# Three edits of order in a hybrid attention, convolution and SSD kernel: when the decay sums are loaded, when four token tiles are finished, and when dt's running sums are formed

## What is computed

```python
u = rmsnorm(h, norm_w[layer])
proj = jnp.einsum('bld,de->ble', u, w_in[layer])
(q, k, v, g_attn, c_b, c_c, c_h, g_conv, z, xbc, dt) = jnp.split(proj, IN_SPLIT_POINTS, axis=-1)
y_attn = diff_attention_branch(q, k, v, ...) * silu(g_attn)       # 4 heads
y_conv = short_conv_branch(c_b, c_c, c_h, ...) * silu(g_conv)
y_ssm = ssd_branch(z, xbc, dt, ...)                               # 4 groups of 4 heads, chunks of 128 tokens
h = h + jnp.einsum('ble,ed->bld', concatenate([y_attn, y_conv, y_ssm]), w_out[layer])
return rmsnorm(h, final_norm_w)[:, N_META:]

# in ssd_branch / ssd_scan
dt = softplus(dt_raw + dt_bias)
acum = jnp.cumsum(a * dt)                  # running sums inside each chunk
seg = acum[..., :, None] - acum[..., None, :]
lmat = jnp.exp(jnp.where(causal, seg, -inf))          # the decay matrix of a chunk
y_diag = (cb * lmat) @ xc
```

## Time and profile before

| | us |
|---|---|
| median of 3 runs (1050.49 to 1052.12) | 1050.74 |
| the profiled execution's own time | 1049.79 |
| its span, first to last instruction | 1048.1 |
| PE busy | 1013.8 (97%) |
| DVE busy | 665.6 (64%) |
| ACT busy | 401.8 (38%) |
| POOL busy | 253.8 (24%) |

### The profile page before, as it was taken

How to read it: one execution, slowest core, us unless ns; L and a number is a source line. 1 busy time by engine, 2 the same in 40 slices (tenths; PEclk the granted TensorE clock), 3 DMA queues, 4 the chain that set the end, 5 groups by cost and what they waited for, 6 DMA issues and landing times.

```text
span 1048.1 us, 16326 instructions
## 1 busy us (share of the span) xinstructions
PE 1013.8 (97%) x6177; PEld 924.9 (88%) x6177; DVE 665.6 (64%) x1327; ACT 401.8 (38%) x892; POOL 253.8 (24%) x222
## 2 busy tenths in 40 slices
PE   4999999999999999999999999999999999999996
PEld 3889989898999898989999989899999898888885
DVE  7555767557257674672576756724767646798866
ACT  6333442233444332334343222343442233544554
POOL 3012331333223312332224133222241330000002
PEclk9999999999999999999999999999999999999999
DMA  8012322221142222211422322114223203994313
GB/s 268 1 44 81 101 81 71 71 61 44 47 133 101 71 81 71 61 41 41 141 84 76 93 71 61 42 41 141 76 70 101 71 20 105 359 389 140 100 51 161
DMA packets 105945, 101.22 MB, mean 97 GB/s; under 512 B 6022, under 2 KB 79852, under 8 KB 105868
## 3 DMA queue, kind: packets, MB, share of 16 engines
q1 hardware_dynamic: 105868, 100.18, 30.0%
HBM read 79.11 MB, written 21.05 MB: 96 GB/s over the span
## 4 chain that ended last, share of the span: by engine, by line
PE 84%; DVE 7%; issue 3%; DMA 2%; ACT 2%; POOL 1%; SPq 0%; POOLq 0%; DVEq 0%; ACTq 0%
PE ps L1599 43%; PE ps L1608 13%; PE ps L1800 9%; PE ps L1584 5%; PE ps L1765 3%; DVE lm_buf L1433 2%; PE ps L1814 2%; DMA acum_b<-acum_scratch 2%; PE ps L1743 2%; PE ps L1744 2%; PE ps L1816 1%; PE ps L1820 1%; PE ps L1691 1%; PE ps L1766 1%; DMA conv_u<-in_norm_w 1%
## 5 line engine op out<-in xcount | busy, mean ns | idle before, releaser
L1599 PE MATMUL ps<-u_hi,w_hi 128*128 128x348 f32 (+3 forms) x1024 | 364.4, 356 | 6.7 <-ACT conv_b_s L1053 2.5
L1599 PE MATMUL ps<-u_lo,w_hi 128*128 128x348 f32 (+3 forms) x1024 | 348.3, 340 | 0.0
L1599 PE MATMUL ps<-u_hi,w_lo 128*128 128x348 f32 (+3 forms) x1024 | 347.7, 340 | 0.0
L1599 PEld LDWEIGHTS ps<-u_hi,w_hi 128*128 128x128 f32 x1024 | 194.0, 189 | 19.8 <-issue 5.5
L904 POOL TENSOR_TENSOR w_lo<-w_raw,w_hi 128x1024 fp32r<-128x1024 f32 (+1 forms) x56 | 123.1, 2197 | 346.2 <-ACT w_hi L994 274.4
L1599 PEld LDWEIGHTS ps<-u_hi,w_lo 128*128 128x128 f32 x1024 | 193.3, 189 | 10.9
L1599 PEld LDWEIGHTS ps<-u_lo,w_hi 128*128 128x128 f32 x1024 | 193.7, 189 | 10.3
L895 POOL TENSOR_TENSOR small<-small,m_half 128x1 f32<-128x1 f32 (+2 forms) x57 | 41.5, 729 | 338.9 <-DVE small L1545 144.8
L1372 DVE TENSOR_REDUCE small<-ps 128x1 f32<-128x144 f32 (+7 forms) x64 | 49.5, 774 | 95.8 <-PE ps L1747 95.3
L1800 PE MATMUL ps<-w_hi,u_hi 128*128 128x256 f32 x256 | 73.1, 286 | 0.0
L1800 PE MATMUL ps<-w_lo,u_hi 128*128 128x256 f32 x256 | 72.0, 281 | 0.0
(11 more groups left out here) (302 smaller groups left out, 1768.7 us busy)
## 6 DMA issues: line engine op xcount, KB each, us to landing
w_raw<-in_w_in SPq DMA_DIRECT2D x56, 512.0 KB, 4.1
acum_b<-acum_scratch SPq DMA_DIRECT2D x32, 256.0 KB, 4.4
acum_b<-in_w_out SPq DMA_DIRECT2D x22, 256.0 KB, 4.3
work<-in_w_out SPq DMA_DIRECT2D x16, 256.0 KB, 4.0
t_scratch<-work SPq DMA_DIRECT2D x16, 256.0 KB, 2.3
t_scratch<-acum_b SPq DMA_DIRECT2D x16, 256.0 KB, 2.6
y_scratch<-ys SPq DMA_DIRECT2D x8, 512.0 KB, 4.0
work<-in_x SPq DMA_DIRECT2D x4, 1024.0 KB, 8.4
```

Source lines behind the costliest of these rows:

```text
L1599: ins = eng.matmul(dst, w[:, k, 0:m], u[:, k, cols], start=(k == 0 and n == 0), stop=(k == KD - 1 and n == 2))
```

## The change

Three edits of order; no instruction is added or taken away, but for the semaphore waits, which move with their steps.

```diff
@@ BEHIND (steps ahead of head 0)
-          ..., *piece(TQ, 1)[:1], ("dt_end", 0), *piece(TQ, 1)[1:], ("lambda_out", 0), ("split", 2), ("load", 3),
-          *piece(TK, 2)[:1], ("dt_cum", 0), ("dt_stat", 0), *piece(TK, 2)[1:], ("split", 3), ("load", 4), ("dt_row", 0), *piece(TV, 0), *piece(TV, 1), *piece(TV, 2)]
+          ..., *piece(TQ, 1)[:1], ("dt_end", 0), *piece(TQ, 1)[1:], ("split", 2), ("load", 3),
+          *piece(TK, 2)[:1], ("lambda_out", 0), *piece(TK, 2)[1:], ("split", 3), ("load", 4), *piece(TV, 0)[:1], ("dt_cum", 0), ("dt_stat", 0), *piece(TV, 0)[1:], *piece(TV, 1), ("dt_row", 0), *piece(TV, 2)]
@@ schedule
     spare(9)
+    add("decay_load", 1)
+    add("decay_load", 2)
     add("z", 4)
...
         f = [slots[c - 1] * w for w in SCAN_SPLIT]
+        if 1 < c and c + 1 < CH:
+            add("decay_load", c + 1)
         if c < CH:
             add("chunk", c)
@@ sync engine
-                    elif step == "decay":
+                    elif step == "decay_load":
                         eng.wait_ge(seg_ok, it * QB + max(a - 2, 0) + 1)
@@ scalar engine, loop over the slots
-                if n == M_22 * KS + 2:
+                if n == M_22 * KS + 1:
                     for t in range(4, QB):
                         square(t, 0)
-            for t in range(QB):
+                if n == M_22 * KS + 4:
+                    for t in range(4):
+                        square(t, 1)
+                if n == M_22 * KS + 7:
+                    for t in range(4):
+                        finish(t)
+            for t in range(4, QB):
                 square(t, 1)
-                if t > 0:
+                if t > 4:
                     finish(t - 1)
@@ vector engine, loop over the slots
-                if (p, j) == (M_22, 7):
+                if (p, j) == (M_22, 6):
                     for t in range(4, QB):
                         first_half(t)
-            for t in range(QB):
-                if t >= 4:
-                    add_bank(M_22, t - 4)
+                if (p, j) == (M_22, 5):
+                    for t in range(4):
+                        mean(t)
+                if (p, j) == (M_22, 7):
+                    for t in range(4):
+                        finish(t)
+            add_bank(M_22, 0)
+            for t in range(4, QB):
+                if t + 1 < QB:
+                    add_bank(M_22, t - 3)
                 mean(t)
-                if t > 0:
+                if t > 4:
                     finish(t - 1)
```

More of the change, by code:

```diff
@@ L180 @@
 BEHIND = [("piece", first_piece(TK)), ("dt_piece", 1), ("piece", first_piece(TQ)), ("dt_piece", 2), *piece(TK, 1)[:1], ("dt", 0), *piece(TK, 1)[1:],
-          ("parameters", 0), ("lambda", 0), ("lambda_end", 0), *piece(TQ, 1)[:1], ("dt_end", 0), *piece(TQ, 1)[1:], ("lambda_out", 0), ("split", 2), ("load", 3),
-          *piece(TK, 2)[:1], ("dt_cum", 0), ("dt_stat", 0), *piece(TK, 2)[1:], ("split", 3), ("load", 4), ("dt_row", 0), *piece(TV, 0), *piece(TV, 1), *piece(TV, 2)]
+          ("parameters", 0), ("lambda", 0), ("lambda_end", 0), *piece(TQ, 1)[:1], ("dt_end", 0), *piece(TQ, 1)[1:], ("split", 2), ("load", 3),
+          *piece(TK, 2)[:1], ("lambda_out", 0), *piece(TK, 2)[1:], ("split", 3), ("load", 4), *piece(TV, 0)[:1], ("dt_cum", 0), ("dt_stat", 0), *piece(TV, 0)[1:], *piece(TV, 1), ("dt_row", 0), *piece(TV, 2)]
 def schedule(last):
```

## The result

| | before | after |
|---|---|---|
| median of 4 runs, us | 1050.88 (1050.49 to 1052.12) | 1043.51 (1043.18 to 1045.58) |
| ratio, with its 95% interval | | 0.9929 (0.9915 to 0.9944) |
| the profiled execution's own time, us | 1049.79 | 1045.58 |
| its span, us | 1048.1 | 1043.9 |

The median of before has one more run than the 1050.74 that the forecast starts from. The profiled execution of after is the slowest of the four: profile against profile shows only 4.2 us.

A forecast was written before the change was run, and what follows sets the result against it. PE, busy 97% of the span, was taken as the bound. Gains of 3.2 + 0.75 + 0.45 - 0.4 = 4.0 us off 1050.74 gave 1046.7 us, with a range of 1044.4 to 1048.4.

The forecast's parts named there:

- Decay loads, heads 0 to 2, 3.2 us: Scan: chunk 4's sums, loaded ahead of the weight load, end three PE stalls on `conv_b_s`, gaining 3.2 us.
- The scan gives it back: Rival: in the scan PE's stall only moves to `conv_u`; sum 0.8 us, time 1049.9; chance 0.13.
- the slower rival: Scan: freed decays run into POOL and PE pays 1.18 us per meeting; 1056.1 us; chance 0.04.
- Head 3, 0.75: Head 3: chunk 8's decay load moves past two of four 256 KB loads, ending a PE wait; gain 0.75 us.
- dt, 0.45: Ahead of dt's sums: PE's 2.30 us stall becomes about 1.85, waiting for V's low weights; gain 0.45 us.
- The join, -1.3: Ahead of joined slots 5 to 7: POOL's four powers each hold DVE 0.41 us, making PE 1.3 us late.
- POOL never gets between DVE's instructions: Rival: slots 5 to 7 start on time, the end gains 0.9 us, sum 5.3; 1045.4 us; chance 0.18.
- The cover: Ahead of joined slots 5 to 7: slack before PE needs slot 7's low halves, put at about 0.3 us.
- The rest of the end, +0.9: After PE's end: the last add following PE at once brings 1.4 us, less 0.5 for output queueing.
- the queueing of the last two outputs: End: the last two 512 KB outputs, issued closer together, queue; a loss of 0.5 us, between 0 and 1.2.
- Three causes carry most of them: PE's waits: two in the scan (2.5 and 2.4 us, each over three), one of 2.3 us ahead of dt's sums.
- my rival of 1047.5: Ahead of joined slots: each power holds DVE POOL's whole 0.61 us, making PE 2.1 us late; chance 0.08.

The follow-up runs named there:

- d_no4: Changed kernel with chunk 4's decay load alone put back behind the weight load in heads 0 to 2; 1046.67 us (ratio 0.9971).
- x_end: Kernel before with only the end's edit (the last product's order) applied; 1048.77 us (ratio 0.9989).
- z_pool: Changed kernel with four further POOL products of 128x256 tiles, one behind each of the four powers at the join; 1044.41 us (ratio 0.9949).
- x_all: Changed kernel with all three edits, run once more beside the single edits; 1043.51 us (ratio 0.9941).
- x_all2: Changed kernel run once more, unaltered, as base for a later set of runs; 1044.37 us (ratio 0.9949).
- z_split: Changed kernel with the split of V's weights put ahead of the copy of q's last piece on ACT; 1044.00 us (ratio 0.9941).
- z_fill: Changed kernel with dt's two sums put ahead of V0 instead of behind its first half; 1042.47 us (ratio 0.9930).
- x_decay: Kernel before with only the decay loads moved; 1046.46 us (ratio 0.9965).
- b_again: Kernel before run once more, unaltered, for a second profile; 1050.04 us (ratio 1.0002).
- x_dt2: Kernel before with only dt's sums moved, run a second time; 1048.26 us (ratio 0.9986).
- z_means: Changed kernel with the four means, and so POOL's four powers, moved from behind slot 5 to behind slot 7; 1043.60 us (ratio 0.9937).
- x_dt: Kernel before with only dt's sums moved, first time; 1048.25 us (ratio 0.9986).

## Why the prediction was wrong, step by step

- **Decay loads, heads 0 to 2, 3.2 us: right.** 632.79 to 629.61 is 3.2 in the two profiles; with dt's or the end's edit alone, at 632.05 to 633.61, it would be 2.4 to 4.0, as chunk 4's load takes from 4.2 to 5.0 us from issue to landing and the stalls on `conv_b_s` 1.7 to 3.3 us in all. Chunk 4 carries it all (d_no4: heads 0 to 2 back at 633.17). PE pays nothing for the 3.39 us; `conv_u` keeps its 2.4. "The scan gives it back" and the slower rival are refuted by the same rows.
- **Head 3, 0.75: right**, 0.8 to 1.0 (234.32 and 234.52 against 233.50 and 233.53), and 0.5 to 0.6 from x_end's 234.06.
- **dt, 0.45: right for the wait, wrong for the edit, which brings 1.86 and 1.98.** The wait went from 2.30 to 1.8 as forecast. The step that failed is that a wait costs its length and no more: in profiles in which the clock falls behind it the stretch takes 1.56 us longer, and the sum had no term for that. The first profile of before did not show it because that execution escaped; one profile was too few to see it. That rarer falls make the other 1.4 to 1.5 us of the median is the likely cause and not a shown one.
- **The join, -1.3: wrong, 0.** The step that failed is that each of POOL's four powers holds DVE 0.41 us; none does. This is the step that I had in doubt, and the rival "POOL never gets between DVE's instructions" gives the right time for it. z_pool shows that the rival's mechanism is not right in general either: POOL does get between, with a cost that goes by POOL's size. What I mis-took was the price of a one-column power from a 256-column row. The cover was too small as well: the forecast's own times, slot 7 at 31.0 and PE at 31.44, give 0.44 and not 0.3, and 0.45 was measured.
- **The rest of the end, +0.9: mis-sized, 1.3** (8.30 to 6.97 in the tail). From PE's end to the last issue it went from 5.29 to 3.35 us, 1.94 gained where I had 1.4, so crowding cost nothing; the queueing of the last two outputs, 0.6, was as I took it (0.5): they land 1.24 us apart and were issued 0.65 apart.
- **The reading of PE's waits.** "Three causes carry most of them" overlooks the two longest, 8.7 and 6.1 us ahead of 50 us. No edit touches them, so no term of the sum rests on it.

In sum: 4.0 as forecast, plus 1.3 (join) and 0.4 (tail), is 5.7 and would still lie in the range; what dt's edit brings beyond 0.45, 1.4 to 1.5 in the medians, carries the time out of it, to 7.1 or 7.2. That this meets the 7.4 so well is partly luck, for x_all and x_all2 gave 6.6 and 5.9 (x_all2 has 1.0 us of wait ahead of the output projection's first slots, which after and x_all have not). Between the profiles of before and after the clock works the other way: 4.0 + 1.3 + 0.4 - 1.56 is 4.1, and they differ by 4.2.

The Trainium skill (SBUF — State Buffer, section Who interferes with whom) has the first of VectorE and GpSimd hold the pair of SBUF ports that they share for a whole instruction. The traces agree: 2.54 us for a DVE instruction of 0.31 behind a POOL instruction of 2.40 (z_split). They do not agree for a power if the first is taken by the start times: it starts 0.05 us ahead of DVE's low half and is the one that is held, 1.75 us. So my rival of 1047.5 fell too: it charged 0.61 us for each power, and each cost DVE nothing.

## What to carry to other kernels

Ask of every stop of PE not only how long it is but whether the clock falls behind it, and look for that in several profiles: here the one profile of before escaped it, and an edit priced at 0.45 us brought 1.9 and 2.0 in the medians. Take the price of a DVE and POOL conflict from a row in which the instruction that comes first has the size of yours; here a helper of one column cost DVE nothing, and a weight split of 2.4 us stopped the instruction beside it that had two inputs in SBUF (z_split) and the decay's four (3.39 us), but not the copies out of PSUM (0.51 us for 344 columns at 62.59 in z_fill, under a `w_lo` that runs to 63.30). And fill a wait with work that is ready (z_fill) before you try to have its cause earlier (z_split), which here moved that cause onto something else.

## What the runs showed of the hardware that was not expected

- PE at half clock behind a stop of 1.8 to 2.3 us: the granted clock is 0.53 or 0.54 over 3.6 us, starting 0.3 us behind the restart (after, x_end) or 1 us behind it (x_decay, b_again), and then full again. Stops of the same length at the same place had no such fall in other executions of the same kernel, and z_split's of 2.44 us had none in its profile.
- In x_decay, b_again, x_dt2, z_split, z_means and z_pool the clock was also low between 16 and 32 us (0.57 to 0.79 over each half of that). No cost is to be seen: they begin q's last piece at 50.49 to 51.17 us, the others at 50.13 to 51.57. PE waits for DVE there for 6.4 us (x_dt2) and 5.2 (x_dt), so it is not what sets the pace. A mean clock of 0.992 against 0.998 tells nothing of the time until it is known where the low stretch lies.
- A POOL power of one column beside a stream of DVE instructions takes 1.75 us (the first of four) or 0.69 (the others) and 0.55 alone, and holds none of them.
